# A hybrid attention trunk on one core: weight pieces alternate over both slots, heads written out, and half of an output product moved in among the heads

## What is computed

```
mod = silu(c) @ w_ada + b_ada            # 9 rows: shift, scale, gate of three sub-layers
x = x + 0.5 * gt1 * swiglu(modulate(rms(x), sh1, sc1), w_ffn1_in, w_ffn1_out)
h = modulate(rms(x), sh2, sc2)
proj = h @ w_in
y_a = forgetting attention, 8 heads of 64, on fq, fk, fv, ff
q, k = silu(conv4(mq)), silu(conv4(mk)); h_b = mLSTM, 4 heads of 128, in chunks
y_b = sigmoid(mo) * rms(h_b) * g_mhn
x = x + gt2 * (concat(y_a, y_b) @ w_out)
x = x + 0.5 * gt3 * swiglu(modulate(rms(x), sh3, sc3), w_ffn2_in, w_ffn2_out)
return rms(x) * g_final
```

## Time and profile before

| what | value |
|---|---|
| median of 3 runs | 2063.83 us (2063.68 to 2064.43) |
| the profiled execution: its own time | 2065.19 us |
| its span, first to last instruction | 2063.5 us |
| mean granted TensorE clock | 0.968 |
| busy share: PE, DVE, ACT, POOL | 93%, 57%, 37%, 43% |
| first part ends, `mixer` ends, second product of the output starts | about 765, 1315, 1356 us |

### The profile page before, as it was taken

How to read it: one execution, slowest core, us unless ns; L and a number is a source line. 1 busy time by engine, 2 the same in 40 slices (tenths; PEclk the granted TensorE clock), 3 DMA queues, 4 the chain that set the end, 5 groups by cost and what they waited for, 6 DMA issues and landing times. The chain is left out here.

```text
span 2063.5 us, 25551 instructions
## 1 busy us (share of the span) xinstructions
PE 1917.5 (93%) x9280; PEld 1568.7 (76%) x9280; DVE 1183.1 (57%) x1682; ACT 763.2 (37%) x1387; POOL 891.1 (43%) x636
## 2 busy tenths in 40 slices
PE   4699999999999969999998997899999999999997
PEld 3488888888888847777777776687788888888886
DVE  5966667655777751444414555448543443548777
ACT  5533233222444431444423444335232333334444
POOL 4887787674000241000012111368977877820002
PEclk8799999999999979999999999899999999999999
DMA  7256565633966201011101111132322323149652
GB/s 290 64 163 199 182 207 173 203 113 123 380 216 194 73 21 42 22 42 42 62 21 41 41 44 41 48 133 77 123 102 96 114 102 110 64 172 364 204 194 82
DMA packets 204616, 257.15 MB, mean 125 GB/s; under 512 B 14014, under 2 KB 124882, under 8 KB 202962
## 3 DMA queue, kind: packets, MB, share of 16 engines
q1 hardware_dynamic: 204498, 255.59, 36.9%
HBM read 206.71 MB, written 48.84 MB: 124 GB/s over the span
## 5 line engine op out<-in xcount | busy, mean ns | idle before, releaser
L420 POOL TENSOR_TENSOR ffn_ring_b<-ffn_raw_in,ffn_ring_b 128x512 fp32r<-128x512 f32 x174 | 247.0, 1426 | 145.1 <-ACT ffn_ring_b L415 145.1
L832 PE MATMUL bank<-ffn_w_hi,ffn_a_hi 128*128 128x512 f32 x616 | 240.1, 390 | 1.2 <-DVE ffn_w_lo L816 1.2
L834 PE MATMUL bank<-ffn_w_hi,ffn_a_lo 128*128 128x512 f32 x616 | 239.7, 389 | 0.0
L833 PE MATMUL bank<-ffn_w_lo,ffn_a_hi 128*128 128x512 f32 x616 | 239.6, 389 | 0.0
L1532 POOL TENSOR_TENSOR mx_w_lo<-mx_raw_w,mx_w_hi 128x1024 fp32r<-128x1024 f32 x29 | 73.0, 2528 | 358.9 <-ACT mx_w_hi L1363 358.8
L415 ACT CAST ffn_ring_b<-ffn_raw_in 128x512 fp32r<-128x512 f32 x174 | 107.9, 621 | 300.2 <-PE bank L1267 284.6
L108 POOL TENSOR_SCALAR rms<-rms 128x1 f32<-128x1 f32 x24 | 15.1, 628 | 444.2 <-ACT ffn_junk L102 430.5
L805 ACT CAST ffn_a_hi<-ffn_a_stage 128x512 fp32r<-128x512 f32 x154 | 95.6, 621 | 202.8 <-PE bank L834 198.5
L1086 DVE TENSOR_TENSOR ffn_u<-bank,ffn_u 128x512 f32<-128x512 f32 x111 | 76.4, 688 | 163.1 <-PE bank L1267 163.1
L1265 PE MATMUL bank<-h_hi,ffn_ring_a_hi 128*128 128x512 f32 x356 | 142.2, 399 | 26.8 <-ACT ffn_g L1014 18.7
L816 DVE TENSOR_TENSOR ffn_a_lo<-ffn_a_stage,ffn_a_hi 128x512 fp32r<-128x512 f32 x154 | 106.4, 691 | 74.5 <-ACT ffn_a_hi L805 74.4
(11 more groups left out here) (316 smaller groups left out, 4694.9 us busy)
## 6 DMA issues: line engine op xcount, KB each, us to landing
ffn_raw_in<-in_w_ffn_in SPq DMA_DIRECT2D x88, 512.0 KB, 5.9
ffn_a_stage<-hidden SPq DMA_DIRECT2D x154, 256.0 KB, 3.4
ffn_w_stage<-in_w_ffn_out SPq DMA_DIRECT2D x132, 256.0 KB, 3.0
ada_rest<-in_w_ada SPq DMA_DIRECT2D x64, 448.0 KB, 4.0
hidden<-ffn_u SPq DMA_DIRECT2D x88, 256.0 KB, 2.0
hidden<-ffn_g SPq DMA_DIRECT2D x66, 256.0 KB, 2.0
mx_raw_w<-in_w_mix_in SPq DMA_DIRECT2D x28, 512.0 KB, 3.8
ada_ring<-in_w_ada SPq DMA_DIRECT2D x8, 1024.0 KB, 12.1
```

The costliest lines, as they stand in the source:

```text
L420: pool.tensor_tensor(self.lo(q), self.source(b, m), self.hi(q).bitcast(F32), ALU.subtract)\
L832: pe.matmul(dst, a_hi, w_hi, start=first, stop=False, skip_group_check=True)
L833: pe.matmul(dst, a_hi, w_lo, start=False, stop=False, skip_group_check=True)
L834: mm = pe.matmul(dst, a_lo, w_hi, start=False, stop=True, skip_group_check=True)
```

## The change

1. **Slots.** The pieces k, q, mo of all heads are numbered m = 0 to 11 and alternate over both slots (`head_w`), so the mo piece of head 0 no longer queues behind its q piece. ACT casts it after the second projection group.
2. **Order within a head.** Heads 1 and 2 are written out. "Turn out" of a head moves behind P4 of the next head. P1' moves from behind the scores to between the transposes of k and the scores. ACT evicts P5 between the two silus and casts the pieces at other places; POOL cuts all three pieces of the next head first and, after its power operation, waits for the normalisation.
3. **Residual parked.** In the first pair of attention heads SP stores `xres` to DRAM (`x_spill`, 8 x 512 KB). Its place in SBUF takes the first 512 tokens of the attention output (`yf_hi`, `yf_lo`), four k of the gated output weights (`wo_raw`, `wo_hi`, `wo_lo`). They are made in heads 1 and 2 on ACT and POOL.
4. **Fillers.** In head 3, `out_fox(k)` computes 12 matmuls of the output product for k = 0 to 3 and token tiles 0 to 3: k = 0, 1 in the place of P0', k = 2 in that of P1', k = 3 in that of P2'. `out_fox_late(t)` computes token tiles 5 and 6 behind the numerators. That is 72 matmuls instead of 24.
5. **After the barrier.** The first half of the product has 120 matmuls in place of 168. The residual comes back by eight loads, four of them before the first weight piece, four after PE has used `wo_hi` for the last time (`first_used`). Pieces n = 2, 3 of the output weights are gated and cut before the barrier, on POOL and ACT.

```diff
-    C_O = (C_M[0] + MH, C_M[1] + 2 * MH)
+    C_O = (C_M[0] + 3 * MH // 2, C_M[1] + 3 * MH // 2)
+    OUT_LATE = (5, 6)
+    def head_w(m):
+        return m % 2, C_M[m % 2] + m // 2
...
+                if first:
+                    for t in range(NS):
+                        sp.dma_start(x_spill[t * P:(t + 1) * P, :], core.xres[:, t, :]).then_inc(x_spilled, 16)
...
+            def gate_wo(piece):
+                w = wo_raw[:, piece, :].rearrange("p (k n) -> p k n", k=2)
+                pool.tensor_tensor(w, w, gate_0[:, :].unsqueeze(1).to_broadcast([P, 2, BANK]), ALU.mult)\
+                    .then_inc(wo_gated, 1)
...
+            for h in range(MH):
+                if h < MH - 1:
+                    for m in range(3 * h + 3, 3 * h + 6):
+                        w_cut_lo(pool, *head_w(m))
+                if h == 1:
...
+                    gate_wo(0)
+                    gate_wo(1)
+                    cut_yf(0)
+                    cut_yf(1)
+                if h == 2:
+                    cut_wo(0)
+                    cut_wo(1)
+                    cut_yf(2)
+                    cut_yf(3)
+                if h == MH - 1:
+                    for k in range(PAIRS):
                         pool.wait_ge(y_hi, k + 1)
                         cut_y_lo(pool, k, y_lo_pool)
+                    for n in range(2, 4):
+                        gate_out(ms, pool, gate_0, n, C_O).then_inc(gated, 1)
                 pool.wait_ge(var_done, h + 1)
...
+                pool.wait_ge(yb_done, h * 2 + 2)
+            for n in range(2, 4):
+                w_cut_lo(pool, n % 2, C_O[n % 2])
...
+                if h == 1:
+                    act.wait_ge(x_spilled, NS * 16)
+                    for k in range(PAIRS):
+                        act.copy(yf_hi[:, k, :], yT_fox[:, k, 0:BANK]).then_inc(yf_hi_done, 1)
+                if h == 2:
+                    for piece in range(2):
+                        act.wait_ge(wo_gated, piece + 1)
+                        act.copy(wo_hi[:, piece, :], wo_raw[:, piece, :]).then_inc(wo_hi_done, 1)
                 if last:
                     act.wait_ge(x_ready, MH * X_PER)
-                    for k in range(2):
-                        act.copy(core.h_hi[:, k, :], yT_fox[:, k, :]).then_inc(y_hi, 1)
+                    for k in range(PAIRS):
+                        act.copy(core.h_hi[:, k, BANK:S], yT_fox[:, k, BANK:S]).then_inc(y_hi, 1)
                 act.wait_ge(args_done, h + 1)
...
                 project(h, 4)
+                if not first:
+                    turn_out(h * 2 - 2)
                 project(h, 5)
                 if not last:
                     project(h + 1, 0)
-                pe.wait_ge(silu_done, h * 2 + 2)
+                else:
+                    pe.wait_ge(x_kept, MH * X_PER)
+                    out_fox(0)
+                    out_fox(1)
+                pe.wait_ge(silu_done, h * 2 + 1)
...
+                if not last:
+                    project(h + 1, 1)
+                else:
+                    out_fox(2)
+                pe.wait_ge(silu_done, h * 2 + 2)
...
-                if not last:
-                    project(h + 1, 1)
                 for j in range(NS - 1):
...
                 if not last:
                     project(h + 1, 2)
+                else:
+                    out_fox(3)
...
-                    for k in range(2):
-                        pe.wait_ge(y_lo_pool, k + 1)
-                        for t in range(NS // 2):
-                            token_product(pe, k, t)
...
+                    pe.wait_ge(o_done, h * 3 + 3)
+                    for t in OUT_LATE:
+                        out_fox_late(t)
+                    turn_out(h * 2)
```

More of the change, by code:

```diff
@@ L1628, in _, with head_load @@
                 w_load(sp, piece % 2, C_MV[0] + piece // 2, w_in[:, 2 * piece:2 * piece + 2, COL_MV:COL_MV + MW])
[L1630 to L1634, removed]
-                if not last:
-                    ml_w(h + 1, 0, COL_MK)
-                if first:
+            def head_load(m):
+                col = m // 3 * P + (COL_MK, COL_MQ, COL_MO)[m % 3]
+                w_load(sp, *head_w(m), w_in[:, :, col:col + P])
+            for m in range(3):
+                head_load(m)
+            for h in range(MH):
+                if h < MH - 1:
+                    head_load(3 * h + 3)
+                if h == 0:
                     sp.wait_ge(y_done, PAIRS * NS)
@@ L1703, in ml_cut @@
                     .then_inc(rpow_done, 1)
-                if not last:
-                    w_cut_lo(pool, 1, h * 2 + (C_M[1] + 3))
-            repeat(pool, MH, ml_cut)
+                pool.wait_ge(yb_done, h * 2 + 2)
+            for n in range(2, 4):
+                w_cut_lo(pool, n % 2, C_O[n % 2])
         @block.scalar
@@ L1851, in ml_body @@
                 act.activation(sq_junk[:, 0:NS], tiny[:, 0, :], ACT.Copy).then_inc(sq_done, 1)
[L1852 to L1855, removed]
                 if not last:
                     keep_x(h + 1, 3, False)
-                    w_cut_hi(act, 1, h * 2 + (C_M[1] + 3), freed=(x_ready, h * X_PER + (X_PER + 4)))
-            repeat(act, MH, ml_body)
+            for h in range(MH):
+                ml_body(h, h == 0, h == MH - 1)
+            for n in range(2, 4):
+                w_cut_hi(act, n % 2, C_O[n % 2], freed=(x_ready, MH * X_PER), is_gated=(gated, n - 1))
         @block.vector
@@ L2079, in ml_body @@
                         .then_inc(yb_done, 1)
-                if last:
-                    cut_y(range(2, PAIRS))
                 for half in range(2):
@@ L2087, in ml_body @@
                         .then_inc(ybt_kept, 1)
-            repeat(dve, MH, ml_body)
+            for h in range(MH):
+                ml_body(h, h == 0, h == MH - 1)
         @block.tensor
@@ L2251, in _, with turn_out, out_fox, out_fox_late @@
                 project(0, g)
+            def turn_out(done):
+                for j in range(NS):
+                    if j % 4 == 0:
+                        pe.wait_ge(yb_done, done + (j // 4 + 1))
+                    mm = pe.transpose(core.bank[:, (7, 4)[j // 4], j % 4 * P:(j % 4 + 1) * P], o_all[:, j, 0:P],
+                                      core.ident[:, :])
+                    if j % 4 == 3:
+                        mm.then_inc(ybt_ready, 1)
+            def out_fox(k):
+                pe.wait_ge(wo_done, k // 2 + 1)
+                pe.wait_ge(yf_done, k + 1)
+                for t in range(NS // 2):
+                    tok, cols = slice(t * P, (t + 1) * P), slice(k % 2 * BANK, (k % 2 + 1) * BANK)
+                    three(pe, core.bank[:, t, :], yf_hi[:, k, tok], yf_lo[:, k, tok],
+                          wo_hi[:, k // 2, cols], wo_lo[:, k // 2, cols], k == 0, False)
+            def out_fox_late(t):
+                for k in range(PAIRS):
+                    pe.wait_ge(y_lo_pool, k + 1)
+                    tok, cols = slice(t * P, (t + 1) * P), slice(k % 2 * BANK, (k % 2 + 1) * BANK)
+                    three(pe, core.bank[:, t, :], core.h_hi[:, k, tok], core.h_lo[:, k, tok],
+                          wo_hi[:, k // 2, cols], wo_lo[:, k // 2, cols], k == 0, False)
             def ml_body(h, first, last):
@@ L2364, in sync @@
         for slot in range(2):
-            sp.wait_ge(ms.w_lo_done[slot], self.C_O[slot] + 4)
+            sp.wait_ge(ms.w_lo_done[slot], self.C_O[slot] + 3)
         self.weights.load(sp, 0)
@@ L2377, in gpsimd @@
         ms, norm, weights, NS = self.ms, self.norm, self.weights, self.c.NS
-        for n in range(1, 8):
+        for n in range(4, 8):
             slot, c = self.at(n)
-            hi, lo = self.out_w(n) if n >= 4 else (ms.w_hi[:, slot, :], ms.w_lo[:, slot, :])
+            hi, lo = self.out_w(n)
             pool.wait_ge(ms.w_hi_done[slot], c + 1)
@@ L2432, in vector @@
                               ALU.subtract).then_inc(self.y_lo, 1)
-        for n in range(2, 8):
+        for n in range(4, 8):
             gate_out(self.ms, dve, self.gate, n, self.C_O).then_inc(self.gated, 1)
```

148 lines of the change are left out of this document (83 added, 65 removed).

## The result

The changed kernel takes **2044.02 us** (median of 4 runs, 2043.35 to 2044.38). The kernel before, run beside it on the same chip, takes 2064.13 (4 runs, 2063.68 to 2066.21). The ratio is 0.990, 95% interval 0.9883 to 0.9917: about 20 us faster. The forecast was 2045.0 in a range of 2035 to 2052. The profiled execution has a span of 2042.6 us against 2063.5, 20.9 less.

What follows compares the result with a forecast made beforehand. PE, busy 93% of the span, was taken as the bound, with gains from its idle or half-rate stretches. Terms -7.6 - 9.2 + 7.6 + 1.3 - 10.9 = -18.8 us gave 2046.4, or 2045.0 for the median; range 2035 to 2052.

Steps and rivals of the forecast that it cites:

- Head 0: First head: mo piece uses the other slot, P4 starts without its wait, N0 at 1144.9 against 1152.53: -7.6 us.
- Heads 1 and 2: "Turn out" no longer waits, DVE and ACT become the bound; two heads take 91.3 against 100.54: -9.2 us.
- Head 3: POOL's cuts and gatings alternate with DVE's chain, so updates start at N2 + 44.6; N2 to N3 52.3 against 44.74: +7.6 us.
- N3 to the barrier: POOL ends last after cutting two pieces; PE starts at N3 + 18.6 against 17.32: +1.3 us.
- Behind the barrier: First half of the output product has 120 matmuls in place of 168, with no wait for weights: -10.9 us.
- Rival 1: Heads 1 and 2: clock falls to half behind the wait before the updates, 4.6 us for both: 2049.6 us; chance 0.24.
- Rival 2: Head 3: POOL and DVE pass each other, so 8.5 us aren't paid: 2036.5 us; chance 0.25.
- Rival 3: Behind the barrier: transfers don't overlap, PE waits 20.7 us and loses 2.3 to the clock: 2068.0 us; chance 0.05.

Runs made afterwards that it cites:

- the late cast: Changed kernel with ACT casting the mo piece of head 0 behind the eviction of P3 instead of P1: 2051.24 us, ratio 0.9934.
- all edits: Changed kernel with the three edits, plus casts of `yf_hi`, `wo_hi` and the next head's q piece behind the exponentials: 2024.51 us, ratio 0.9806.
- three edits: Changed kernel with casts of `h_hi` behind the exponentials, DVE's copies behind the convolution of k, POOL's two cuts behind the barrier: 2025.25 us, ratio 0.9813.

## Why the prediction was right

**Head 0, -7.6:** -7.6 measured. P4 follows P3 without a gap, and the late cast gives the gain back (8.0 us from P0 to N0).

**Heads 1 and 2, -9.2:** -8.8. N to N was put at 45.65 and is 45.98 and 45.77. The bound was named rightly: DVE, held by the copies of the turned output. Its convolutions start at N + 16.8 (predicted 17.05), and moving the copies takes the waits almost away. ACT's casts cost the 0.7 assumed. The prediction priced the groups of these heads at full clock and so had a gain in its sum that it didn't name: from N0 to N2 the mean granted clock was 0.95 before (half clock for 10.2 us around and behind the waits before "turn out", in 9.0 of which PE worked) and is 1.00 now, which makes some 4.5 of the 8.8 us. PE alone was put at 43.5 per head (N + 35.0 and 8.5) and is 43.8 in the run with all edits. The wait was 1.7 rather than 2.1; another 0.98 before the transposes of the scores (L2366), where before there was 0.6 at most, had not been counted.

**Head 3, +7.6:** +4.8. This is the term that was mis-sized; its mechanism is shown by three runs (ACT's casts moved, POOL's cuts and gatings held back, the gatings alone held back). Two parts of the step were off in size. The updates start at N2 + 42.8, not + 44.6: the short chain ends at N2 + 36.4 instead of + 37.35, `sg` and `arg` together take 5.0 instead of 5.6, since the first gating had begun at 1272.01, 1.1 us ahead of the chain's end, and `kw` 1.4 instead of 1.6. PE's wait there was put at about 12 us; it is 8.4, with 1.75 more at the first filler (1259.93). And from the updates to N3 it took 6.8, not 7.7: the clock was back 2.9 us after the updates had begun, where before it took 4.4 us, so that `out_fox(3)` ran at full speed. This 0.9 is luck of the profiled execution: with the same code in this stretch it took 8.0 us in the run with the late cast, 7.3 in that with the casts of `yf_hi` and `wo_hi` moved and 7.0 in that with POOL's cuts behind the barrier.

```profile
1281.00:1282.00 1.00, 1.00 (x6) 1.00 (x6) 0.70 (x2) 0.00 (x0) 0.00 (x0) 0.50 0.00 0
1282.00:1283.00 1.00, 1.00 (x9) 0.93 (x8) 0.70 (x2) 0.00 (x0) 0.00 (x0) 0.82 0.00 0
1283.00:1284.00 1.00, 1.00 (x9) 0.91 (x8) 0.79 (x3) 0.31 (x1) 0.00 (x0) 1.00 0.00 0
```

These are windows of the changed kernel (columns as in the earlier trace rows). The sum of -18.8 stands against -21.3 over these stretches and -20.9 in the span. Head 3 alone is off by 2.8, and heads 1 and 2 take 0.4 of it back. That the forecast for the median was off by only 1.0 is in part luck: it took 1.36 off for a profiled execution that lay above its median, and that of the changed kernel lies only 0.3 above its own.

**N3 to the barrier, +1.3:** +1.1. POOL is last: its two cuts end at 1303.37, DVE's copies at 1300.1. That these could go behind the barrier for nothing was not seen.

**Behind the barrier, -10.9:** -10.8. The piece that was said to be ready at B + 24 to 26.5 is ready at B + 27.5, with 2.2 us to spare instead of 3.

**Rival 1 (clock falls in heads 1 and 2)** did not occur. In all windows of 1 us around the updates of these heads the granted clock is 1.00, behind waits of 1.74, 1.55 and 0.98 us. The rival was nearer than this looks. The wait was put at 2.1 us, and behind waits of 2.13 to 2.18 us the clock fell to 0.50 all three times in the run with "turn out" back; the waits came out at 1.7 and 1.6. The rule of the Trainium skill, "TensorE: Matmul & The Clock Gate", Part 1, that a short gap by itself doesn't throttle, agrees with the changed kernel's heads and not with that run.

**Rival 2 (POOL and DVE pass each other)** did not occur in the changed kernel but does with "turn out" back in its place, and N2 to N3 is 6.25 us shorter there, a part of it because DVE starts its convolutions 2.4 us sooner. The margin was small: POOL's first cut came 0.3 us ahead of the first short step in the changed kernel, and 1.8 us behind it in that run.

**Rival 3 (transfers don't overlap)** fell. Over the stretch behind the barrier most microseconds move 350 to 420 GB/s, and the issues read, with KB and us to landing:

```profile
xres<-x_spill SPq DMA_DIRECT2D x8, 512.0 KB, 5.3
mx_raw_w<-in_w_mix_out SPq DMA_DIRECT2D x4, 512.0 KB, 5.9
```

Whether parking the residual costs something that other work hides was not tried: a kernel without the stores and loads has no room for the operands of the fillers.

## What to carry to other kernels

When two engines share a memory and one of them has a chain of tiny steps on the critical path, look at what the other is released to do beside it: a few bulk instructions cost the chain as many full lengths as it has steps, and holding them back by one wait gave 7 us here. Ask what releases them: if it is the chain itself, starting the chain sooner brings both, and doesn't help. When a wait is moved, count the clock behind it too: here an exchange of 2.15 us for 1.7 kept 1.7 us of clock per head. And a stage that ends in a barrier should carry ahead of it nothing that an idle stretch behind it can take.

## What was not expected of the hardware

- **Who is blocked depends on the operation.** DVE's steps with operands in SBUF alone, even those of 128x8, lasted until POOL's instruction ended (1.04 to 2.30 us for 0.17). The scores (L2092 in the run where POOL waits for `kw`), with one operand in PSUM, took their usual 1.28 us right beside POOL's cuts:

```profile
1270.87 1.28 DVE L2092 SCALAR_TENSOR_TENSOR mx_dec<-bank,mx_dec 128x512 f32<-128x512 f32 x2
```

```profile
1270.49 4.97 POOL L1543 TENSOR_TENSOR h_lo<-mx_yT_fox,h_hi 128x512 fp32r<-128x512 f32 x4 [24.48 <-DVE mx_kw L2085]
```

  The Trainium skill, "GPSIMD Engine Reference", 1. Specifications, says that GpSimd's contention is with those VectorE instructions that run in a 2-port mode or have two SBUF inputs. The trace agrees for the scores and for the blocked steps with two SBUF inputs; it adds that the length of the instruction is no protection. The scales of `sg` and `arg` were blocked with one tensor input in SBUF; whether they run in a 2-port mode no run here shows.
- **The clock at the barrier isn't told by the wait's length alone.** Behind the same 1.98 us it stayed at 1.00 in the run with POOL's cuts behind the barrier and in that with three edits (first matmul 0.47 us), and fell to 0.50 in the run with all edits (0.77 us) and 30.0 us to the second product against 27.3:

```profile
1286.82 0.77 PE L2542 MATMUL bank<-mx_wo_hi,h_hi 128*128 128x512 f32 x1 [1.98 <-PEq L65]
```

Behind 5.28 us it fell in every profile. The profiled execution with all edits was the slowest of its four (2027.13), and that of the three edits the fastest (2024.0). The 2 to 4 us by which the runs of these kernels differ can be this fall, 2.7 us, or the stretch ahead of the heads, which differs by 1.4 us between these two profiles. What decides the clock stayed open.
